# Decode attention spread over two other stages: steps between the projection's blocks and between the prompt attention's parts

## The reference, cut to what matters

```python
z      = rmsnorm(x) @ w_in                      # 15 column blocks: q, k, v, gates, decay, ...
s      = q1 @ k1.T, q2 @ k2.T                   # two score maps for each head
attn   = softmax(s1) - lam * softmax(s2)        # differential attention, prompt rows
dec    = the same for 8 sequences x 4 tokens over cache_k, cache_v through page_table
gla    = gated linear attention over the prompt and the samples, with a state
y      = x + concat(norm(attn) * gate, norm(gla) * gate) @ w_out
```

## Time and profile before

| | us |
|---|---|
| three runs | 1261.6, 1264.76, 1267.02 (median 1264.76) |
| profiled execution, span | 1259.8 |
| PE busy in the span | 1038.3 (82%) |
| DVE, ACT, POOL busy | 584.6, 490.0, 254.2 |
| projection | 0 to 421.5 |
| decode attention | 421.5 to 816 |
| prompt attention | 816 to 1018 |
| GLA | 1018 to 1151 |
| output product | 1151 to 1259.8 |

### The profile page before, as it was taken

The page is one execution under the profiler, slowest core; times in us unless marked ns, Lnnn a source line. Parts: engine busy times, 40 slices in busy tenths (PEclk is TensorE's granted clock), DMA queues, the critical chain, the costliest instruction groups (busy, mean ns, idle before and its releaser), DMA issues. The chain is left out here.

```text
span 1259.8 us, 27242 instructions
## 1 busy us (share of the span) xinstructions
PE 1038.3 (82%) x9055; PEld 868.5 (69%) x9055; DVE 584.6 (46%) x1430; ACT 490.0 (39%) x1383; POOL 254.2 (20%) x399
## 2 busy tenths in 40 slices
PE   4999999999999487879878887467788836777998
PEld 4999999997999466556655654155667625664886
DVE  4755522302222134443443443277878458868221
ACT  5644314613424223333333432156767345533110
POOL 0000000000000222343434341222211159800000
PEclk9999999999999799999999998558999967787999
DMA  5312332212111699999999999530000052102221
GB/s 169 93 38 95 106 122 80 82 34 76 53 49 49 215 386 338 385 387 387 387 387 387 387 387 169 148 111 9 17 10 13 1 175 74 51 26 69 97 89 60
DMA packets 106820, 195.21 MB, mean 155 GB/s; under 512 B 14406, under 2 KB 48652, under 8 KB 106732
## 3 DMA queue, kind: packets, MB, share of 16 engines
q1 hardware_dynamic: 85716, 126.03, 30.8%
q0 software_dynamic: 20480, 67.13, 14.3%
q10 hardware_dynamic: 536, 0.89, 0.2%
HBM read 174.41 MB, written 19.60 MB: 154 GB/s over the span
## 5 line engine op out<-in xcount | busy, mean ns | idle before, releaser
L843 POOL DMA_DIRECT2D vraw<-in_cache_v x256 | 137.6, 537 | 667.7 <-issue 663.8
L512 PE MATMUL pz<-wh,xTh 128*128 128x256 f32 (+1 forms) x864 | 248.7, 288 | 0.0
L512 PE MATMUL pz<-wh,xTl 128*128 128x256 f32 (+1 forms) x864 | 244.3, 283 | 0.0
L512 PE MATMUL pz<-wl,xTh 128*128 128x256 f32 (+1 forms) x864 | 244.2, 283 | 0.0
L925 PE MATMUL pk<-ident,kraw 128*128 128x128 f32 x1024 | 136.7, 291 | 57.0 <-DMA kraw<-in_cache_k 54.0
L925 PEld LDWEIGHTS pk<-ident,kraw 128*128 128x128 f32 x1024 | 121.8, 150 | 70.9 <-DMA kraw<-in_cache_k 62.0
L863 DVE COPY kt<-pk 128x512 f32<-128x512 f32 x128 | 82.9, 687 | 183.1 <-PE pk L925 182.1
L512 PEld LDWEIGHTS pz<-wh,xTh 128*128 128x128 f32 (+1 forms) x864 | 160.6, 186 | 1.6 <-issue 1.2
L512 PEld LDWEIGHTS pz<-wh,xTl 128*128 128x128 f32 (+1 forms) x864 | 160.7, 186 | 0.0
L512 PEld LDWEIGHTS pz<-wl,xTh 128*128 128x128 f32 (+1 forms) x864 | 160.5, 186 | 0.0
L643 DVE SCALAR_TENSOR_TENSOR wl<-wraw,nw,wh 128x256 fp32r<-128x256 f32 x112 | 52.3, 482 | 117.1 <-ACT wh L358 116.2
(11 more groups left out here) (241 smaller groups left out, 1857.5 us busy)
## 6 DMA issues: line engine op xcount, KB each, us to landing
kraw<-in_cache_k SPq DMA_DIRECT2D x256, 256.0 KB, 9.6
vraw<-in_cache_v POOLq DMA_DIRECT2D x256, 256.0 KB, 5.7
wraw<-in_w_in SPq DMA_DIRECT2D x14, 1024.0 KB, 5.6
out<-nat SPq DMA_DIRECT2D x32, 128.0 KB, 1.8
xb<-in_x_prompt SPq DMA_DIRECT2D x7, 512.0 KB, 3.6
xr<-in_x_prompt SPq DMA_DIRECT2D x7, 512.0 KB, 3.5
out<-xr SPq DMA_DIRECT2D x7, 512.0 KB, 2.6
val_d<-nat SPq DMA_DIRECT2D x16, 128.0 KB, 1.8
```

What stands on the lines that cost most here:

```text
L512: ins = pe.matmul(z_at(u)[0:r, 0:CB], a[:, k, P * i:P * i + r], b[:, c % 2, k, :], start=(n == 0), stop=(n == 3 * KT - 1))
L843: pool.dma_start(vraw[:, g % VR, n, :], cache_v.rearrange("a n p h d -> (a n) p (h d)")[bass.ds(page, 1)] .rearrange("o p c -> (o p) c")). ...
```

## The change

- The stages are now: projection with decode steps in it, GLA, prompt attention with the rest of the decode steps, output.
- Decode attention is written as one generator for each engine. A *tick* is what was a group of 4 pages, in 8 steps; a sequence takes 9 ticks. `steps_at(u)` says up to which step the engines go behind use u of the projection: from row tile 4 of block 4 on, 4 steps behind each of 18 uses, then about 7.1 behind each of 62 uses, until step 512 of 665. These cover 228 of the 256 key pages. The remaining 153 steps follow a list `plan` between the parts of the prompt attention.
- The rings shrink: `kraw` from 16 to 6 pages, `vraw` from 32 to 8, `kt` to 6. The projection has 3 banks in place of 4, decode has two for turned keys (one page each, even pages copied by ACT, odd by DVE), one for scores, turned exponentials and the final gather, one for the products with the values. `wraw` is loaded in halves.
- Queries and the split keys go to DRAM (`q_d`, `ks_d`) in the projection and come back in the prompt attention by POOL's queue; the split of the keys is done by DVE in the projection, `query_lo` by POOL alone.
- In the prompt attention, scores have two banks (`low2`) that both maps of a large unit share, and the turn has one bank. For a large unit `before = 2 * u + m`, so the second map's scores wait for the first map's exponentials.
- `w_out` is loaded at the end of the prompt attention.

```diff
-NZ = 4
+NZ = 3
...
+        KR, VR, TR = 6, 8, 6
...
+        RG = G + 1
+        SUBS = 8
+        NSUB = (NB + 1) * RG * SUBS + 2 * SUBS + 1
+        PAUSE = (7 * RG + 1) * SUBS
...
+        def decode_sp(sp):
+            def load_key(p):
+                if p >= KR:
+                    sp.wait_ge(kt_done, p - KR + 1)
+                page = sp.value_load(pages[0:1, p:p + 1], min_val=0, max_val=POOL - 1)
+                sp.dma_start(kraw[:, p % KR, :],
...
+                    for n in range(GRP):
+                        yield
+                        if kb is not None and t < G:
+                            p = kb * NPAGES + t * GRP + n + KR
+                            if p < NP:
+                                load_key(p)
+                        yield
...
+            def steps_at(u):
+
+                if u not in paced:
+                    return 0
+                n, slow = paced.index(u) + 1, paced.index(("n", 6, 4))
+                if n <= slow:
+                    return GRP * n
+                return GRP * slow + (PAUSE - GRP * slow) * (n - slow) // (len(paced) - slow)
...
+            pTb, pO = bank[:, 2, :], bank[:, 3, :]
+            low2, high3 = [bank[:, a:b, :].rearrange("p a x -> p (a x)") for a, b in ((0, 2), (4, 7))]
...
+                        before = 2 * u + m - (1 if small(u) else 0)
+                        if before > 0:
+                            pe.wait_ge(exp_done, before)
```

More of the change, by code:

```diff
@@ new lines, in hymba_kernel @@
+        bank = ps(ctx, "bank", [P, 8, 512])
+        nat_stored = [sem(f"nat_stored{n}") for n in range(3)]
+        pages_in = sem("pages_in")
+        skew_out = sem("skew_out")
+        g_out = sem("g_out")
+        band_out = sem("band_out")
+        c_zero = sem("c_zero")
+        nt_out = sem("nt_out")
+        klo_done = sem("klo_done")
+        st_out = [sem(f"st_out{n}") for n in range(3)]
+        st_stored = [16 * sum((1 if t < 2 * TILES else 2) for t in range(4 * TILES) if t % 3 == n) for n in range(3)]
@@ new lines, in decode_pool, with load_value @@
+        def decode_pool(pool):
+            def load_value(p):
+                if p >= VR:
+                    b, g = (p - VR) // NPAGES, (p - VR) % NPAGES // GRP
+                    pool.wait_ge(pv_done, b * RG + g + 2)
+                page = pool.value_load(pages[0:1, p:p + 1], min_val=0, max_val=POOL - 1)
+                pool.dma_start(vraw[:, p % VR, :],
+                               cache_v.rearrange("a n p h d -> (a n) p (h d)")[bass.ds(page, 1)]
+                               .rearrange("o p c -> (o p) c")).then_inc(v_in[p % VR], 16)
+            pool.wait_ge(pages_in, 16)
+            pool.wait_ge(skew_out, 16 * H)
+            for r in range(NB + 2):
+                _, b, _ = row_of(r)
+                for t in range(ticks(r)):
+                    for n in range(SUBS):
+                        if b is not None and t >= 1 and n < GRP:
+                            load_value(b * NPAGES + (t - 1) * GRP + n)
+                        yield
@@ L181, in hymba_kernel @@
             LOGS = GA + 1
+            BLOCKS = [c for c in range(len(KINDS)) if c != GA]
+            wslot = lambda c: BLOCKS.index(c) % 2
             CH = [(0, 384), (384, 384), (768, NTOK - 768)]
@@ L348, in x_hi, with w_hi @@
                            .then_inc(xhi_done, 1)
[L350 to L358, removed]
+                def w_hi(c, at=range(KT)):
+                    if at[0] == 0 and c >= 2:
+                        act.wait_ge(z_done, BLOCK_END[BLOCKS[BLOCKS.index(c) - 2]])
+                    for k in at:
+                        x = half_of(c, k)
+                        act.wait_ge(w_loaded[x % 2], 16 * (x // 2 + 1))
+                        act.activation(wh[:, wslot(c), k, :], raw(c, k), ACT.Copy, scale=nw[:, k:k + 1])\
                            .then_inc(whi_done, 1)
@@ L2084, in hymba_kernel @@
+        with ExitStack() as st:
+            m_ = Area(nc, FREE, SB_HIGH)
+            woh = m_.take("woh", [P, KT, D], F32R)
+            wol = m_.take("wol", [P, KT, D], F32R)
+            mh = m_.take("mh", [P, 2, KT, P], F32R)
+            ml = m_.take("ml", [P, 2, KT, P], F32R)
+            xr = m_.take("xr", [P, 2, D])
+            pY = [bank[:, n, :] for n in range(4)]
             xr_in = [sem(f"xr_in{n}") for n in range(2)]
```

2009 lines of the change are left out of this document (1073 added, 936 removed).

## The result

The changed kernel takes 1430.55 us (1428.6 to 1443.81, 4 runs), the kernel before 1265.89 in the same comparison: 1.132 times as long, interval 1.126 to 1.138. The direction was forecast, the size was not: 1294 in a range up to 1345. The profiled span is 1427.8 us.

The account below looks back on a forecast made before the run. Transfers were taken to bound decode attention, PE the projection. 1264.8 - 394.5 + 228 + 66 + 44 + 59 + 25 + 4 - 5 + 3 gave 1294 us, 2.3% slower, range 1190 to 1345.

Parts of the forecast that it names:

- Decode work in the projection, +228 "at PE's pace": Projection: PE takes on the moved decode work at an undisturbed group's 3.88 us for 4 pages, nothing hiding it; +228 us.
- Key loads that come late, +66: Projection's gate uses: key loads queue behind the store of `nat`, so PE waits 4.1 us a use; +66 us.
- a rival at 0.15: Gate blocks and large units: gaps lower PE's granted clock, work some 20% longer, 24 + 16 us, about 1335; chance 0.15.
- the main case: Whole kernel: the summed terms hold, 1294 us, own range 1271 to 1320; chance 0.38.
- Other waits, +44: Projection: waits for ACT's copies 12, three banks and the decay's step in `gv` blocks 22, sequence ends 10; +44 us.
- Large units, +59: Prompt attention's large units: the second map's scores come only after the unit's chain of work, lengthening each unit; +59 us.
- Small units +25: Prompt attention's small units: 8 decode ticks, 31 us of PE, with a third of PE's idle time absorbing some; +25 us.
- rounded queries -5: Prompt attention: half of the query subtractions leave DVE, the busiest engine of the small units; -5 us.
- start +3: Prompt attention's start: loads of queries and keys, with POOL alone now doing work ACT and DVE did; +3 us.
- GLA 0: GLA stage: the same work, alone as before, so no change; 0 us.
- tail 0: Prompt attention's tail, 29.0 us: no growth counted; loading `w_out`, 12 us, fits under it.
- the 147 us on offer: Decode attention: transfers make it 394.5 us long, PE needs 248 for 256 pages; hiding the transfers offers about 147 us.

Follow-up runs that it names:

- e1: Changed kernel, with SP issuing a use's key loads ahead of its wait for `nat` instead of behind the store: 1359.69 us (1.075).
- e12: On e10, PE's order within every tick becomes two turns, all scores, values, two turns: 1260.31 us (0.994).
- e13: On e10, the order of e12 for ticks in the projection alone, the old order in the prompt attention: 1248.35 us (0.987).
- e10: Changed kernel with the edits of e1, e3, e5 and e6, and DVE making half of row tile 0's rounded queries: 1260.52 us (0.996).
- e3: Changed kernel, a large unit's second map getting the two banks of the turned keys, its scores again ahead of turns: 1362.7 us (1.078).
- e8: Kernel before the change, with the edit of e5 alone (band's copies made from DRAM): 1249.11 us (0.989).
- e6: On e1, DVE does a use's decode copies ahead of the next weight's rounding and the row block before: 1348.85 us (interval 1.059 to 1.075).
- e9: Changed kernel with the edits of e1, e3, e5 and e6, and ACT's decode work ahead of its activations: 1287.05 us (1.015).
- e2: Changed kernel, with the band's four stores issued by POOL's queue instead of SP's: 1433.77 us.
- e5: Changed kernel, with the band stored to DRAM once and its four copies made from there: 1403.74 us.

## Why the prediction was too low

- **Decode work in the projection, +228 "at PE's pace": the step that failed most.** PE is busy for 711.5 us up to 863, where 399.6 + 228 = 628 were forecast: 84 more. The pace came from one undisturbed group, 3.88 us for 4 pages. But over its whole stage, at a clock of 0.91, PE was busy for 301.7 us for 256 pages. By pages that makes 269 for 228, so about half of the miss stood in the row that was read first. The other half is an assumption: that the mixture leaves the projection's own instructions as they were.
- **The same 84 by kind of work.** For each PE instruction in the traces, count the time from its start to its end, or to the next one's start if that comes first. Decode's instructions then take 275 us of the 711.5 and all others 436: 47 and 37 more than forecast. Without the late key loads (e1) these two are 12 and 15 less, the low clock's 27. Cutting decode into pieces costs too: a page turned alone takes 0.60 (at 348.88 above), four in a row took 1.97, and with larger pieces decode's part is about 237 (e12, e13) in place of 254 (e10). Of the others' 37, 20 stay in e13, at a clock of 0.98: a use's products between decode steps take about 3.1 us where 2.88 stood before. Why they do was not tested.
- **Key loads that come late, +66: right in mechanism, too large in size.** The term was waiting alone, and PE waited for `kraw` for 47 us, 43 by e1. With the clock's 27, which is counted in the 84 above, the late loads cost 70; that this is near 66 is chance. The clock had been a rival at 0.15, to be had in place of the main case; it was a part of it, since with the gaps gone (e1) the slow products were mostly gone too.
- **The band's stores: a term that was missing.** 27 us. The change moves these stores into the projection, which the prediction did not price, and the trace before showed what they cost: from 770 to 780 the transfer engines had a share of 0.88 and moved 33 GB/s. The tail of the decode stage was taken as the end of a pipeline and not asked for its cause.
- **Other waits, +44:** 51 measured, but in other places, so that the sum is near is luck. The three banks cost 3.3 us in the `gv` blocks and not 22; the copies 44 and not 12; the sequences' ends 4.1 and not 10.
- **The projection in sum:** 84 + 27 + 7 less the 19 by which the wait for `kraw` was overestimated are 99 of the 103 that it was longer than forecast.
- **Large units, +59: right in mechanism, and without the clock.** They grew by 84 (93 to 177), and undoing it gave 68. PE idles for 52.7 us of the 177 where it idled for 13.7 of 93, 39 more, so the waits for `e` and the turn's copy came, but for less than 59. Its busy time grew by 45 (79.3 to 124.3, decode's value steps among it), and 35 of that went with the clock, from 0.80 to 1.00, in e3.
- **Small units +25, rounded queries -5, start +3:** from 816 to 896 before and from 1003 to 1101 now, 80 and 98 us, so +18 where 23 were forecast. PE's first scores come 14 us into the stage; before, they came 9 us into it.
- **GLA 0 and tail 0: wrong by 7 and 12 us.** GLA's first wait of PE, for `ff`, is 21.3 us where 15.0 stood before. In the tail PE waits 5.3 us for `e` in place of 2.6, at a clock of 0.75 in place of 0.94, and the last turn of `mix_b` with its wait of 4.8 falls into it, which before came at 1020, behind the boundary. The tail stays at 39 with e3, so the large units' banks are not its cause; its own three banks, which both maps share now, were left as they are. Neither was tested further.

The Trainium skill (TensorE: Matmul & The Clock Gate, HAM oscillation — how this bites in real kernels) describes work that waits for a transfer in every round and starts each round throttled, so that a wait is paid twice. This trace agrees: 3.7 us of waiting, then products of 5.3 us and not 2.9; without the wait they ran at 2.9 to 3.1 nearly everywhere.

Where did the 147 us on offer go? The repaired kernel (e13) by stage, projection, GLA and prompt attention:

```profile
0.00:742.70 742.70, 657.68 (x6434) 560.44 (x6434) 297.06 (x843) 274.86 (x787) 103.55 (x196) 0.98 0.66 205
742.70:884.00 141.30, 86.21 (x603) 71.20 (x603) 103.19 (x233) 53.18 (x173) 78.32 (x112) 0.75 0.19 58
884.00:1134.30 250.30, 192.59 (x1586) 141.10 (x1586) 133.78 (x325) 143.63 (x415) 93.08 (x113) 0.92 0.49 155
```

Its projection ends at about 743 where 421.5 + 228 = 650 were possible, GLA takes 141 us in place of 133, and the prompt attention, with the other 28 pages in it, 250 in place of 202. The kernel before with its band mended (e8) needs 1249 as well. Most of the transfers that were to be hidden are hidden (PE waits for `kraw` for 21.9 us in e13, where it waited 54.0 in the decode stage of before), and PE pays for hiding them: 658 us busy in the projection where 628 were reckoned.

## What to carry to other kernels

Work that is placed into another stage's gaps should be priced by what the mixture costs PE, waits and the clock behind them together, and not at the pace it has alone. Such a price is read from the whole stage that goes, and not from its best group. In a shared queue, ask of each load which semaphore its neighbour ahead waits for: e1 moved the loads ahead of such a wait and gave 71 us, and in e6 and e9, where other work went ahead of `nat`, waits for the same loads came back. And a stretch of the trace before in which the transfer engines are busy and move little is worth a question of its own: here it was worth 1.1% with four new lines and one changed, and the whole rebuilding, with that edit in it, 1.3%.

## What the runs showed of the hardware

Four stores of 192 KB that each read one row of on-chip memory 128 times landed after 9.5 to 25.0 us on SP's queue and after 10.4 to 29.1 on POOL's (e2), and while SP's were under way some 28 GB/s were moved in all; the same copies read from DRAM landed after 3.2 to 4.7 us (e5). The granted clock could not be read from the busy share: with PE busy for 124 of 177 us it was 0.80 in the large units, and with 13.3 of 20 it was 1.00 in the decode stage of before. What tells the two apart stays open.
